# Duos of several parts in a fused two-block transformer: query blocks 0 and 2 share one, compressed parts ride with block 1's

## The reference, cut to what matters

```
# A: 4 heads with two maps each; B: 8 heads, window 128, a sink; C: 8 heads, three branches
s = einsum('bqhcd,bkhcd->cbhqk', qi, k) * scale + bias          # A, causal
p = softmax(where(mask, s, NEG_INF)); w = p[0] - lam * p[1]; out = w @ v
...
p_cmp = where(cmask, softmax(where(cmask, q . kc * scale, NEG_INF)), 0)   # C, 31 compressed keys
o_cmp = p_cmp @ vc
o_sel = softmax(q . ks * scale + bias) @ vs                       # C, selected blocks (all 8 of 8)
o_win = banded_attention(q, kw, vw, bias_tab, C_WINDOW)           # C, window 512
out = g0 * o_cmp + g1 * o_sel + g2 * o_win
```

## Time and profile before

| | |
|---|---|
| median of 3 runs | 3474.31 us (3467.3 to 3478.09) |
| profiled execution | 3464.92 us |
| its span | 3463.1 us |
| PE busy | 3352.8 us, 97% |
| DVE busy | 1709.9 us, 49% |
| ACT busy | 1342.5 us, 39% |
| POOL busy | 2099.7 us, 61% |
| mean TensorE clock granted | 0.991 of full speed |

### The profile page before, as it was taken

The page is one execution under the profiler, slowest core; times in us unless marked ns, Lnnn a source line. Parts: engine busy times, 40 slices in busy tenths (PEclk is TensorE's granted clock), DMA queues, the critical chain, the costliest instruction groups (busy, mean ns, idle before and its releaser), DMA issues.

```text
span 3463.1 us, 50722 instructions
## 1 busy us (share of the span) xinstructions
PE 3352.8 (97%) x19962; PEld 2833.2 (82%) x19962; DVE 1709.9 (49%) x3322; ACT 1342.5 (39%) x2839; POOL 2099.7 (61%) x1242
## 2 busy tenths in 40 slices
PE   7888999999999999999999999999999999999999
PEld 6655777988899899767779999998997677789998
DVE  6554342465546666442224667566755432236444
ACT  3656552322233434254322443443342543224333
POOL 7514447676676467554667556755675546675565
PEclk9999999999999999999999999999999999999999
DMA  3212223235424452222233455235522222232232
GB/s 143 69 62 88 71 62 104 92 125 197 182 74 175 173 188 86 75 74 69 85 95 98 151 192 194 86 119 210 189 98 74 68 67 85 83 107 98 98 104 80
DMA packets 108269, 388.62 MB, mean 112 GB/s; under 512 B 12400, under 2 KB 12784, under 8 KB 98816
## 3 DMA queue, kind: packets, MB, share of 16 engines
q1 hardware_dynamic: 88272, 292.76, 25.4%
q10 hardware_dynamic: 19760, 92.62, 7.4%
HBM read 383.20 MB, written 2.13 MB: 111 GB/s over the span
## 4 chain that ended last, share of the span: by engine, by line
PE 82%; DVE 7%; DMA 4%; ACT 4%; POOL 1%; issue 1%; ACTq 0%; DVEq 0%; POOLq 0%
PE psum L1472 18%; PE psum L1474 17%; PE psum L1473 17%; PE psum L1541 7%; PE psum L1543 7%; PE psum L1542 7%; DMA ada_t<-ada_dram 4%; PE psum L1580 2%; PE psum L1622 2%; DVE ada_t L2218 2%; PE psum L1597 2%; DVE rs_t L2086 1%; PE psum L1566 1%; POOL w_lo L1428 1%; POOL w_hi L1425 1%
## 5 line engine op out<-in xcount | busy, mean ns | idle before, releaser
L1425 POOL TENSOR_TENSOR w_hi<-raw,ones 128x1024 fp32r<-128x1024 f32 (+2 forms) x437 | 745.4, 1706 | 679.8 <-PE psum L1474 671.9
L1428 POOL TENSOR_TENSOR w_lo<-raw,w_hi 128x1024 fp32r<-128x1024 f32 (+2 forms) x437 | 943.3, 2159 | 34.3
L1440 POOL TENSOR_TENSOR w_hi<-raw,w_hi 128x512 fp32r<-128x512 f32 x312 | 403.3, 1307 | 549.7 <-ACT w_hi L1725 545.0
L1472 PE MATMUL psum<-h_hi,w_hi 128*128 128x512 f32 (+2 forms) x1704 | 664.5, 390 | 24.2 <-DVE r L2102 9.4
L1474 PE MATMUL psum<-h_hi,w_lo 128*128 128x512 f32 (+2 forms) x1704 | 626.4, 368 | 0.0
L1473 PE MATMUL psum<-h_lo,w_hi 128*128 128x512 f32 (+2 forms) x1704 | 626.1, 367 | 0.0
L1472 PEld LDWEIGHTS psum<-h_hi,w_hi 128*128 128x128 f32 (+1 forms) x1704 | 323.4, 190 | 111.7 <-issue 40.8
L1472 PE MATMUL psum<-a_hi,w_hi 128*128 128x512 f32 (+1 forms) x1064 | 392.6, 369 | 0.0
L1473 PE MATMUL psum<-a_lo,w_hi 128*128 128x512 f32 (+1 forms) x1064 | 392.0, 368 | 0.0
L1474 PE MATMUL psum<-a_hi,w_lo 128*128 128x512 f32 (+1 forms) x1064 | 391.8, 368 | 0.0
L1474 PEld LDWEIGHTS psum<-h_hi,w_lo 128*128 128x128 f32 (+1 forms) x1704 | 323.4, 190 | 56.0
(11 more groups left out here) (233 smaller groups left out, 6194.5 us busy)
## 6 DMA issues: line engine op xcount, KB each, us to landing
raw<-weights_dram SPq DMA_DIRECT2D x487, 512.0 KB, 3.6
ada_t<-ada_dram ACTq DMA_DIRECT2D x72, 1024.0 KB, 6.1
raw<-weights_dram SPq DMA_DIRECT2D x76, 256.0 KB, 2.6
raw<-weights_dram SPq DMA_DIRECT2D x32, 384.0 KB, 3.7
bias_t<-biases_dram ACTq DMA_DIRECT2D x36, 256.0 KB, 3.0
bias_t<-cum_dram ACTq DMA_DIRECT2D x16, 256.0 KB, 3.7
out_dram<-x SPq DMA_DIRECT2D x8, 256.0 KB, 2.0
raw<-weights_dram SPq DMA_DIRECT2D x4, 408.0 KB, 3.2
```

Source lines behind the costliest of these rows:

```text
L1425: nc.gpsimd.tensor_tensor(high, piece, ones[:, 0:1].to_broadcast([P, n]), ALU.mult)\
L1428: nc.gpsimd.tensor_tensor(w_lo[:, p % NR, 0:n], piece, high.bitcast(F32), ALU.subtract)\
L1440: nc.gpsimd.tensor_tensor(low_of(op), src, high_of(op).bitcast(F32), ALU.subtract)\
L1472: mm(dst, lh, rh, start=first, stop=False)
```

## The change

A duo now has a list of parts, each with its own query block, branch and width; a part has its columns in the duo's score banks and its chunks in the transposed tile. Blocks 0 and 2 of a pair share a duo in att_a, att_a2 and att_c2 (128 + 384 columns, or 1 + 3 blocks), block 3 and block 1 have their own; att_b keeps one duo per block. In att_c the win parts of blocks 0 and 2 share a duo, and the sel parts another; block 3 has two, and block 1 has two, with the compressed parts of blocks 0 and 1 in its win duo and of 2 and 3 in its sel duo. Odd pairs go through the list backwards, except in att_c. Score, minima, exps, inverses, prob, turn and pv loop over the parts; one semaphore step ends each of score, turn, copy and pv of a duo, as before. The row tiles grow from 4 to 12 columns. In att_a the exps of half 1 wait until the minima of all parts are done.

```diff
+BLOCKS = dict(att_a=((0, 2), (3,), (1,)), att_b=((0,), (3,), (1,), (2,)), att_a2=((0, 2), (3,), (1,)),
+              att_c2=((0, 2), (3,), (1,)))
+COMPRESSED = dict(win=(0, 1), sel=(2, 3))
+def parts_of(kind):
+    if kind == "att_c":
+        duos = [[Part(i, br, 0, i + 1) for i in own] for own in ((0, 2), (3,), (1,)) for br in ("win", "sel")]
+        for duo in duos[-2:]:
+            duo += [Part(i, "cmp", 0, 0) for i in COMPRESSED[duo[0].br]]
+        return duos
+    los = [max(0, i - 1) if kind == "att_b" else 0 for i in range(TB)]
+    return [[Part(i, "one", los[i], i + 1 - los[i]) for i in own] for own in BLOCKS[kind]]
 def duos_of(kind, layer):
...
-        for i in ((0, 3, 1, 2), (2, 1, 3, 0))[pair % 2]:
-            brs = [("win", i + 1), ("sel", i + 1), ("cmp", 0)] if kind == "att_c" else [("one", i + 1 - lo)]
+        parts = parts_of(kind)
+        if pair % 2 and kind != "att_c":
+            parts.reverse()
+        duos = [Duo(kind, layer, pair, own, False, False, bias) for own in parts]
@@ attend
-        w = 1 + max([d.blocks for d in duos[max(0, j):j + 3]])
+        w = 1 + max([d.chunks for d in duos[max(0, j):j + 3]])
@@ score
-                for half in TWO:
-                    k = kc_sb[rows, :] if u.br == "cmp" else region[where][rows, chunk, u.lo * P:u.lo * P + w]
-                    ins = mm(bank(SCORE_BANKS[half], w), q, k, start=True, stop=u.kind != "att_c2")
+                for p in u.parts:
+                    for half in TWO:
+                        q = region[Q_AT[u.kind]][rows, u.pair, p.i * P:(p.i + 1) * P]
...
+                        ins = mm(scores_at(u, p, half), q, k, start=p.column == 0, stop=u.kind != "att_c2",
+                                 skip_group_check=True)
@@ exps
+                for n, p in enumerate(u.parts):
+                    for half in TWO:
+                        E.wait_ge("row_min", u.rows if u.kind == "att_a" and half else u.turn(n, half))
+                        s, r = s_sb[:, u.at + half, p.column:p.column + p.width + sink_of(u)], u.row(n, half)
@@ inverses
+                for n, p in enumerate(u.parts):
+                    for half in TWO:
+                        E.wait_ge("exps", u.turn(n, half))
...
                 if u.kind == "att_a":
-                    E.wait_ge("first_map", u.n)
+                    for n, p in enumerate(u.parts):
+                        E.wait_ge("first_map", u.mapped - len(u.parts) + n + 1)
@@ pv
+                for p in u.parts:
+                    o = O_BANK * S + p.i * P
+                    for b in range(p.chunks):
+                        first, last = u.first and p.turned + b == 0, p.stop and b == p.chunks - 1
```

More of the change, by code:

```diff
@@ L472, with width, chunks @@
 @dataclass(eq=False)
+class Part:
+    i: int
+    br: str
+    lo: int
+    blocks: int
+    column: int = 0
+    turned: int = 0
+    stop: bool = False
+    @property
+    def width(self):
+        return CMP_N if self.br == "cmp" else self.blocks * P
+    @property
+    def chunks(self):
+        return max(1, self.blocks)
+@dataclass(eq=False)
 class Duo:
@@ L477 @@
     pair: int
[L478 to L483, removed]
+    parts: list
     first: bool
@@ L494, with __post_init__, chunks @@
     out: int = 0
+    def __post_init__(self):
+        column = turned = 0
+        for p in self.parts:
+            p.column, p.turned = column, turned
+            column += p.width
+            turned += p.chunks
     @property
     def width(self):
-        return CMP_N if self.br == "cmp" else self.blocks * P
+        return sum(p.width for p in self.parts)
+    @property
+    def chunks(self):
+        return sum(p.chunks for p in self.parts)
     @property
@@ L1603, in pv @@
                 E.wait_ge("pt_copied", u.n)
[L1604 to L1605 removed]
+                if any(p.br == "cmp" for p in u.parts):
                     E.wait_ge("vc_done", 1)
[L1607 to L1623, removed]
+                v = values[V_AT[u.kind]]
@@ L1785, in exps @@
             def exps(u):
[L1787 to L1794, removed]
+                for n, p in enumerate(u.parts):
+                    for half in TWO:
+                        E.wait_ge("row_min", u.rows if u.kind == "att_a" and half else u.turn(n, half))
+                        s, r = s_sb[:, u.at + half, p.column:p.column + p.width + sink_of(u)], u.row(n, half)
+                        to = scores_at(u, p, half) if u.kind == "att_a" and half else s
+                        fn(to, s, ACT.Exp, scale=-1.0, bias=row_min[:, r:r + 1], accum_out=row_sum[:, r:r + 1])\
+                            .then_inc(sem["exps"], 1)
@@ L1817, in copy @@
                     E.wait_ge("pv", u.n - 1)
-                rows, w = (CMP_N, P) if u.br == "cmp" else (P, u.width)
+                w = u.chunks * P
+                rows = CMP_N if all(p.br == "cmp" for p in u.parts) else P
                 if u.kind == "att_a":
```

180 lines of the change are left out of this document (102 added, 78 removed).

## The result

The changed kernel takes 3434.71 us (median of 4 runs, 3424.84 to 3441.23), against 3472.07 for the kernel before (median of 4 runs, 3467.3 to 3478.09): a ratio of 0.9889, 95% interval 0.9858 to 0.992. That is 37.4 us less; forecast were 29. The profiled execution took 3441.23 us, near the upper end of its runs.

A forecast was written before the change was run, and what follows sets the result against it. PE's own work was taken as the bound nearly everywhere (busy 97% of the span), with an ACT and DVE chain limiting places in att_a. Terms 24.4 + 4.7 + 3 - 3 = 29 us off 3474.3 gave 3445; range 3428 to 3466.

The forecast's parts named there:

- its own signs: Trace signs: att_c 15 to 18 us shorter, att_a2 and att_c2 2 to 3 us shorter each time, among others.
- Steps on PE in att_c: att_c: 24 fewer duos at 0.56 us save 13.4 us, less 1.2 for compressed pv parts changing shape.
- Ends of att_c: Start and end of att_c: evenly dealt fill covers PE's stalls and part of the clock loss; 4.7 us, bounds 0 and 6.6.
- att_a: 3 from waits and 1.6 from steps: att_a: fewer engine round trips gain 3 us (bounds -5 and 15); four fewer score steps on PE gain 1.6.
- The wait for the last probability step: att_a: PE's score waits for the previous duo's probabilities, 15.2 us in 11 times, should sum to less.
- the roots' reciprocals: att_a: reciprocals of the normed projections hold DVE for 34.0 us and stay; the argument against stalls going entirely.
- Layers: att_c2 and att_a2, each run twice: eight fewer duos save 4.5 us at 0.56 and 6.1 us at 0.76.
- Longer blocks on ACT and DVE: All stages: longer exps and reciprocals delay work queued behind them; 3 us lost, bounds 0 and 60.
- The first (fixed cost per part): All attention on PE: fixed cost goes with the part, not the step; gain 13.6 us, 3461; chance 0.15.
- The second (3431, stalls go entirely): att_a gives 12 us, att_c's ends 6.6, ACT and DVE lose nothing; gain 43 us, 3431; chance 0.10.
- The third (slower): att_c: the two fill banks come free too late, 62 us lost in place of 3; 3504; chance 0.07.
- The fourth: Whole kernel: no change, as steps PE saves come back as waits; 3474; chance 0.08.

## Why the prediction was right

The direction, the place and the mechanism that carries most of the gain (fewer steps on PE) were right; 3445 was 10.3 us above the median, and the stages give 38.8 us where the terms sum to 29. Two of its own signs were passed: att_c is 20.6 us shorter where 15 to 18 were named, the layers' attentions 3.5 to 3.9 where 2 to 3 were.

*Steps on PE in att_c: 12.2 predicted, 11.9 found.* With idle time taken out, PE's order of time has the scores at 29.3 before and 25.0 after, pv at 28.5 and 25.8, the fill at 153.2 and 144.6, turns at 18.1 and 19.0. That is some 15 less, of which 3.1 is the slower clock that PE ran at before. The 0.9 lost at the turns I had priced at nothing.

*Ends of att_c: 4.7 predicted, 8.7 found.* This is the term that was off most. I let 5.1 us of fill take 2.0 of the 3.1 us at the start and half of the clock's loss. All 5.6 us of idle time went, and the clock's loss of 3.1 in full: 8.7, above the bound of 6.6. The bound left out that the clock had dropped behind the start's stalls too. A window of the kernel before there (columns as above):

```profile
322.00:326.00 4.00, 2.96 (x10) 2.14 (x8) 1.61 (x12) 2.74 (x11) 0.00 (x0) 0.57 0.00 0
```

2.96 us of PE at 0.57 is worth some 2.96 x 0.43 = 1.3 us, beside the 1.7 of the earlier trace rows.

*att_a: 3 from waits and 1.6 from steps predicted, some 4 found over att_a and att_b.* That the sizes agree is luck. PE's steps gave 3.4 us, twice their term, which counted the score's share alone; idle time and clock together gave 0.6 on average between four profiles without the merge and six with it, well within their spread. The wait for the last probability step was to be under 15.2 us and is 16.5 (14.2 to 15.2 in the four, 15.9 to 17.3 in the six): the waits per trip got longer as the trips got fewer. The wait for the copy fell in exchange, from 2.7 to 4.2 us to 0.6. I named the roots' reciprocals as what stays, and taking them out changed the stage by no more than its spread. What did hold part of it is a line that I dealt with in a half sentence, and for att_c only: the bias loads ahead of ACT's copy. ACT's wait at them is 8.8 us in all four profiles without the merge and 13.9 in all six with it, and moving them gave 4 to 6 us.

*Layers: 4.5 predicted for att_c2 and 6.1 for att_a2, 7.2 and 7.4 found.* In att_a2 the steps gave 3.1 us each time, 0.78 for a duo where I had 0.76; what is beyond is the lower clock, 1.0 to 1.4 us less of it, with 0.6 more of idle time. In att_c2 the steps gave 3.0, 0.75 for a duo and not 0.56, and idle time 0.6. The causal mask's matmuls of att_c2 (128*128) stand between score and pv, and I didn't count them; that they are the difference is argued, no run took it apart.

*Longer blocks on ACT and DVE: 3 lost predicted, none found* where PE is the bound. No fill matmul in att_c waits for sig or the merge product.

*Rivals.* The first (fixed cost per part) falls by the two-part score of 1.06 us and by the two runs on it, the split score (0.2 us a change) and the met wait (nothing). The second (3431, stalls go entirely) came nearer to the median than the forecast did: att_c's ends were as it had them, and the reason that I held against it, the reciprocals, is not borne out by the run without them; but att_a's 12 us did not come with this change. Only the bias load and the scale, moved, bring some 4 to 6 and 3.7 of them. The third (slower) has no trace anywhere. The fourth falls with att_c.

## What to carry to other kernels

Where PE is the bound and its matmuls use the array in several shapes, count the changes of shape: here each cost 0.1 to 0.2 us, so several small products of one shape belong together. An instruction that waits in an in-order queue holds all that stands behind it, so a DMA that waits for a buffer to come free belongs behind the work that doesn't need it. Taking work off an engine tells whether that engine sets a stage's length more surely than its busy share does. And a stage's gain is best split into idle time, clock and the rest before it is put down to a cause: att_a's length alone looked like less waiting, and the split shows steps.

## What was not expected of the hardware

- A wait on a semaphore that had long been met, put between matmuls of one shape on PE, cost nothing that 24 of them in att_c could show (214.23 against 214.25 us).
- A short stall can cost more than its length: the 5.6 us of idle time around att_c's ends came with 3.1 us lost at a lower granted clock, 0.57 in a 4 us window behind each end's stall, where the changed kernel, whose PE doesn't stand still there, has 1.00. It doesn't always: with the compressed parts in duos of their own, 4.9 us of idle time in att_c left the clock at 1.00 throughout. What decides it isn't shown.
- With 19 us of DVE's work taken out of att_a, the stage got no shorter beyond its spread, and the next one 14 us longer, as idle time and lower clock. Why, and why att_a's merged duo last loses 8 us, stay unexplained, as does the spread of 893 to 909 us in the stretches between the attentions.
